# A two-block decoder in one kernel: the first transfers and splits in smaller pieces, the first chunks serving both token tiles, small loads after chunk 9, the last token tile's left half first, two output queues

## The reference

```python
def _rmsnorm(t, g):
    t32 = t.astype(jnp.float32)
    t32 = t32 * lax.rsqrt(jnp.mean(t32 * t32, axis=-1, keepdims=True) + RMS_EPS)
    return t32.astype(t.dtype) * g

def _swiglu(t, w_gate, w_up, w_down):
    return (jax.nn.silu(t @ w_gate) * (t @ w_up)) @ w_down

# first steps of the first layer
f = _swiglu(_rmsnorm(h, ffn1_pre_g[l]), ffn1_w_gate[l], ffn1_w_up[l], ffn1_w_down[l])
h = h + 0.5 * _rmsnorm(f, ffn1_post_g[l])
...
# last steps of the last layer
h = h + conv_ffn(rms_norm(h, ffn_norm[layer]), ffn_w_up[layer], ffn_conv[layer], ffn_w_down[layer])
...
return rms_norm(h, final_norm)
```

## Time and profile before

| | |
|---|---|
| timed runs | 1845.45 us median (1845.1 to 1845.69) |
| the profiled execution: span, first to last instruction | 1842.3 us (its time beyond the span is not listed) |
| TensorE busy | 1829.0 us, 99% |
| VectorE, ScalarE, GpSimd busy | 1287.1, 1090.7, 205.1 us |
| the chain that ended last | TensorE 96%, VectorE 2%, ScalarE 1% |
| DMA | 333.94 MB, mean 181 GB/s |

### The profile page before, as it was taken

One profiled execution on the slowest core, in us unless ns is written; L12 is line 12 of the kernel. 1 busy time (PEld: TensorE's weight loads), 2 busy tenths in 40 slices (PEclk: granted clock), 3 DMA queues, 4 the chain that ended last, 5 costly groups with the idle time before them and its releaser, 6 DMA issues.

```text
span 1842.3 us, 28823 instructions
## 1 busy us (share of the span) xinstructions
PE 1829.0 (99%) x10951; PEld 1633.5 (89%) x10951; DVE 1287.1 (70%) x2041; ACT 1090.7 (59%) x1885; POOL 205.1 (11%) x158
## 2 busy tenths in 40 slices
PE   8999999999999999999999999999999999999998
PEld 7888999998888888888999888888889998989997
DVE  6775747787777568755777788755768765768763
ACT  7665545555666466645555657655557654757653
POOL 0220001110022002200011102210002210001210
PEclk9999999999999999999999999999999999999999
DMA  9755565455576558664654548654747654537663
GB/s 268 216 186 183 172 194 171 140 158 176 173 225 192 189 148 233 186 193 139 196 176 143 186 146 230 193 190 144 226 139 215 187 195 155 173 115 205 198 192 103
DMA packets 435721, 333.94 MB, mean 181 GB/s; under 512 B 25338, under 2 KB 381312, under 8 KB 435584
## 3 DMA queue, kind: packets, MB, share of 16 engines
q1 hardware_dynamic: 435008, 331.57, 59.7%
q10 hardware_dynamic: 576, 0.53, 0.1%
HBM read 330.97 MB, written 1.05 MB: 180 GB/s over the span
## 4 chain that ended last, share of the span: by engine, by line
PE 96%; DVE 2%; ACT 1%; issue 0%; DMA 0%; ACTq 0%
PE bank L1759 16%; PE bank L1736 15%; PE bank L1738 15%; PE bank L1737 15%; PE bank L1747 7%; PE bank L1761 7%; PE bank L1748 7%; PE bank L1749 7%; PE bank L1765 2%; PE bank L1758 1%; DVE wlo L1106 1%; PE bank L2017 0%; DVE U L1159 0%; PE bank L2083 0%; PE bank L2088 0%; PE bank L2054 0%
## 5 line engine op out<-in xcount | busy, mean ns | idle before, releaser
L1106 DVE TENSOR_TENSOR wlo<-raw,whi 128x1024 fp32r<-128x1024 f32 (+3 forms) x637 | 760.9, 1202 | 286.3 <-ACT whi L578 276.8
L578 ACT ACTIVATE whi<-raw 128x1024 fp32r<-128x1024 f32 (+3 forms) x637 | 645.6, 1023 | 324.6 <-PE bank L1738 247.9
L1759 PE MATMUL bank<-U,whi 128*128 128x512 f32 x1280 | 439.2, 395 | 0.2 <-DVE wlo L1106 0.2
L1761 PE MATMUL bank<-U,wlo 128*128 128x256 f32 x1120 | 314.6, 281 | 0.0
L1747 PE MATMUL bank<-U,whi 128*128 128x256 f32 x1024 | 289.2, 282 | 0.0
L1748 PE MATMUL bank<-U,whi 128*128 128x256 f32 x1024 | 286.1, 279 | 0.0
L1749 PE MATMUL bank<-U,wlo 128*128 128x256 f32 x1024 | 286.0, 279 | 0.0
L1759 PEld LDWEIGHTS bank<-U,whi 128*128 128x128 f32 x1280 | 230.2, 188 | 42.9 <-DVE wlo L1106 0.7
L1736 PE MATMUL bank<-whi,U 128*128 128x384 f32 (+2 forms) x592 | 219.2, 370 | 2.7 <-DVE wlo L1464 2.1
L1736 PE MATMUL bank<-whi,hhi 128*128 128x512 f32 x560 | 219.3, 392 | 0.0
L1738 PE MATMUL bank<-wlo,hhi 128*128 128x512 f32 x560 | 218.1, 390 | 0.0
(11 more groups left out here) (309 smaller groups left out, 2367.4 us busy)
## 6 DMA issues: line engine op xcount, KB each, us to landing
raw<-in_ffn_w_up SPq DMA_DIRECT2D x351, 256.0 KB, 3.5
raw<-in_ffn_w_down SPq DMA_DIRECT2D x264, 256.0 KB, 2.9
raw<-in_ffn_w_gate SPq DMA_DIRECT2D x175, 256.0 KB, 3.4
raw<-in_w_gate SPq DMA_DIRECT2D x128, 192.0 KB, 2.9
raw<-in_w_in SPq DMA_DIRECT2D x80, 256.0 KB, 3.4
raw<-in_a_w_in SPq DMA_DIRECT2D x48, 256.0 KB, 3.2
raw<-in_w_mem_kv SPq DMA_DIRECT2D x32, 256.0 KB, 3.3
raw<-in_w_out SPq DMA_DIRECT2D x32, 256.0 KB, 3.1
```

What stands on the lines that cost most here:

```text
L578: act.activation(whi[n % SLOTS][:, 0:w], raw[n % RAW][:, 0:w], ACT.Copy).then_inc(hi_ready, 1)
L1106: dve.tensor_tensor(wlo[n % SLOTS][:, 0:w], raw[n % RAW][:, 0:w], whi[n % SLOTS][:, 0:w].bitcast(F32), ALU.subtract).then_inc(lo_ready, 1)
L1759: ins = pe.matmul(dst, wh, u2[:, k, :], start=(k == 0), stop=(k == KT - 1))
L1761: pe.matmul(dst[:, 0:TOK], wl, uhi[:, k, :], start=False, stop=False)
```

## The change

At the head:
- x comes in four pieces of 128 x 512. The order on SP is: identity, x tile 0 left, the second half of chunk 0, x tile 1 left, chunk 1, x tile 0 right, x tile 1 right, chunks 2 and 3. ScalarE loads the first half of chunk 0.
- The 16 small loads are issued after the DMAs of chunk 9. The ones are made by a memset of VectorE instead of a load.
- TensorE does the gains' transpose first, then 7 fillers, the transposes of x tile 0 left, 9 fillers, x tile 1 left; the right halves are transposed behind chunk 1.
- Chunks 0 to 3 are each used for both token tiles before the next one, and all four are split in halves of 512 columns. High and low parts of x are made two k at a time, and ScalarE reads a bank again (odd j) once VectorE is done with the two k before.
- Three load semaphores become one (`p_loaded`, 15 loads), and the counts of `lo_ready` and `hi_ready` follow the halves.

At the end, token tile 1 gets its left half from all four last chunks and then its right half; VectorE multiplies each half by the gain as soon as it is summed; after the reciprocal ScalarE scales columns 0 to 383 and stores them itself, VectorE columns 384 to 1023, which SP stores.

```diff
+        halves_done = lambda c: 2 * c + 2 if c < 4 else c + 5
+        LAST = 10
+        BY_ACT, BY_DVE = slice(0, 384), slice(384, DM)
...
                 if c >= RAW:
-                    sp.wait_ge(lo_ready, c - RAW + 2)
+                    sp.wait_ge(lo_ready, halves_done(c - RAW))
...
                     for s in range(2):
                         load(c + 2 * m + s, cols(w[s], KT, m * P, P))
+                    if m == 4 and after:
+                        after()
...
             sp.dma_start(ident, consts[:, C_ID:C_ID + P]).then_inc(cst_loaded, 16)
-            sp.dma_start(H[:, 0, :], A["x"][0, ts[0], :]).then_inc(x_loaded[0], 16)
+            load_x(0, 0)
             g0, u0 = A["ffn1_w_gate"][0], A["ffn1_w_up"][0]
+            chunk0 = raw[0][:, :].rearrange("p (k s n) -> p k s n", k=2, s=2)
+            for j, w in enumerate((g0, u0)):
+                sp.dma_start(chunk0[:, 1, j, :], w[P:2 * P, 0:256]).then_inc(w_loaded[0], 16)
+            load_x(1, 0)
             load(1, both(g0, u0, 2, 0))
+            load_x(0, 1)
+            load_x(1, 1)
             load(2, both(g0, u0, 4, 0))
-            sp.dma_start(H[:, 1, :], A["x"][0, ts[1], :]).then_inc(x_loaded[1], 16)
             load(3, both(g0, u0, 6, 0))
...
+            def small_inputs():
+                sp.dma_start(cst[:, C_GT:C_COS], consts[:, C_GT:C_COS]).then_inc(cst_loaded, 16)
+                sp.wait_ge(par_tp, 1)
...
+                if l == 0:
+                    ffn(0, 4, small_inputs)
...
@@ ScalarE
+            act.wait_ge(consts_ready, 2)
+            first_high(0, 0)
+            first_split(0)
+            first_high(1, 0)
+            first_high(0, 1)
+            first_high(1, 1)
+            first_split(1)
+            first_high(0, 2)
+            first_high(1, 2)
+            first_split(2)
+            first_high(0, 3)
+            first_high(1, 3)
+            first_split(3)
+            h_squares(0, 0)
+            split_to(4)
+            h_squares(0, 1)
             split_to(5)
...
+            act.activation(xn[:, 1, BY_ACT], xn[:, 1, BY_ACT], ACT.Copy, scale=stat(LAST, 1, RSTD)).then_inc(xn_done, 1)
+            act.wait_ge(xn_done, 4 * len(norm_at) + 1)
+            act.dma_start(out[0, ts[1], BY_ACT], xn[:, 1, BY_ACT]).then_inc(y_stored, 16)
...
@@ VectorE (the head in the same order as ScalarE, with first_low for first_high and h_bias for h_squares)
+            for nb in range(2):
+                wait_f(LAST, 1, nb)
+                dve.tensor_tensor(H[:, 1, half[nb]], bank[acc(LAST) + 2 + nb][:, :], H[:, 1, half[nb]], ALU.add).then_inc(h_ready, 1)
+                dve.wait_ge(h_ready, 4 * post(LAST) + 2 + nb + 1)
+                dve.tensor_tensor(xn[:, 1, half[nb]], H[:, 1, half[nb]], gpost[:, half[nb]], ALU.mult).then_inc(scaled, 1)
...
+            dve.tensor_scalar(xn[:, 1, BY_DVE], xn[:, 1, BY_DVE], stat(LAST, 1, RSTD), None, ALU.mult).then_inc(y_out, 1)
...
@@ TensorE
+                if b == 0:
+                    stream_turn(0, 1, 0)
                     for j in range(4):
+                        for t in range(TT):
+                            ins = token_block(c + j, j, t, 0, bank[t][:, :], 512, uh, ul, lambda k: first_operands(t, k))
...
+                            if j == 1:
+                                stream_turn(0, t, 1)
...
-            keep_busy(12)
             pe.wait_ge(pre_loaded, 16)
             pe.transpose(bank[0][:, 0:2 * KT], param_rows[0:2 * KT, 0, :], ident[0:2 * KT, 0:2 * KT]).then_inc(par_tp, 1)
-            keep_busy(4)
-            for nb in range(2):
-                stream_turn(0, 0, nb)
-            keep_busy(6)
-            pe.wait_ge(par_ready, 1)
+            keep_busy(7)
+            stream_turn(0, 0, 0)
+            keep_busy(9)
+            pe.wait_ge(consts_ready, 2)
```

More of the change, by code:

```diff
@@ L231, in program @@
         hi_ready, lo_ready, w_used = sem("hi_ready"), sem("lo_ready"), sem("w_used")
[L232 to L235, removed]
+        cst_loaded, pre_loaded, p_loaded = (sem(n) for n in ("cst_loaded", "pre_loaded", "p_loaded"))
+        x_loaded, x_rest, c0_loaded = [sem(f"x_loaded{t}") for t in range(TT)], sem("x_rest"), sem("c0_loaded")
+        gp_loaded, gb_loaded, rot_loaded = (sem(n) for n in ("gp_loaded", "gb_loaded", "rot_loaded"))
+        par_tp, consts_ready = sem("par_tp"), sem("consts_ready")
         f_full = sem("f_full")
@@ L401, in both, with ffn @@
                 return pieces
-            def ffn(f, skip=0):
+            def ffn(f, skip=0, after=None):
                 l, n = f // 2, f % 2 + 1
@@ L427, in _ @@
[L427 to L434, removed]
@@ L517, in _ @@
             conv_ffn(1)
-            for t in range(TT):
-                for nb in range(2):
[L520 to L526, removed]
+            for nb in range(2):
+                sp.wait_ge(y_out, nb + 1)
+                sp.dma_start(out[0, ts[0], half[nb]], xn[:, 0, half[nb]]).then_inc(y_stored, 16)
+            sp.wait_ge(y_out, 3)
+            sp.dma_start(out[0, ts[1], BY_DVE], xn[:, 1, BY_DVE]).then_inc(y_stored, 16)
             sp.wait_ge(y_stored, 64)
@@ L812, in mixer, with first_high, first_split @@
                 split_to(w0 + 3 + SLOTS)
[L815 to L827, removed]
+            def first_high(t, j):
+                if j % 2:
+                    act.wait_ge(u_done, 4 * (j - 1) + 2 * t + 2)
+                for k in (2 * j, 2 * j + 1):
+                    act.wait_ge(ut_full, (2 * (j // 2) + t) + 1)
+                    src = bank[acc(0) + 2 * t + j // 2][:, (k % 4) * P:(k % 4 + 1) * P]
+                    act.activation(uhi[:, k, ts[t]], src, ACT.Copy, scale=par[:, k:k + 1]).then_inc(uhi_done, 1)
+            def first_split(n):
+                for h, s in enumerate(half):
+                    if n == 0 and h == 0:
+                        act.wait_ge(c0_loaded, 32)
+                    else:
+                        act.wait_ge(w_loaded[n], 32)
+                    act.activation(whi[n][:, s], raw[n][:, s], ACT.Copy).then_inc(hi_ready, 1)
+                split[0] = n + 1
+            act.wait_ge(consts_ready, 2)
[14 more added lines that the diff above has]
+            h_squares(0, 1)
             split_to(5)
@@ L1456, in mixer, with first_low, first_split @@
                 split_to(w0 + 3 + SLOTS)
+            dve.memset(ones, 1.0).then_inc(consts_ready, 1)
             dve.wait_ge(par_tp, 1)
[L1460 to L1472, removed]
+            dve.tensor_copy(par[:, 0:2 * KT], bank[0][:, 0:2 * KT]).then_inc(consts_ready, 1)
+            def first_low(t, j):
+                dve.wait_ge(uhi_done, 4 * j + 2 * t + 2)
+                for k in (2 * j, 2 * j + 1):
+                    src = bank[acc(0) + 2 * t + j // 2][:, (k % 4) * P:(k % 4 + 1) * P]
+                    dve.scalar_tensor_tensor(ulo[:, k, ts[t]], src, par[:, k:k + 1], uhi[:, k, ts[t]].bitcast(F32),
+                                             ALU.mult, ALU.subtract).then_inc(u_done, 1)
+            def first_split(n):
+                for h, s in enumerate(half):
+                    dve.wait_ge(hi_ready, 2 * n + h + 1)
+                    dve.tensor_tensor(wlo[n][:, s], raw[n][:, s], whi[n][:, s].bitcast(F32), ALU.subtract).then_inc(lo_ready, 1)
+                split[0] = n + 1
+            first_low(0, 0)
+            first_split(0)
+            first_low(1, 0)
+            first_low(0, 1)
+            first_low(1, 1)
+            first_split(1)
+            first_low(0, 2)
+            first_low(1, 2)
+            first_split(2)
+            first_low(0, 3)
+            first_low(1, 3)
+            first_split(3)
+            h_bias(0, 0)
+            split_to(4)
+            h_bias(0, 1)
             split_to(5)
@@ L1712, in _ @@
             conv_ffn(1)
[L1714 to L1724, removed]
+            residual(LAST, 0, lambda nb: wait_f(LAST, 0, nb))
+            h_bias(LAST, 0)
+            h_rstd(LAST, 0)
+            dve.wait_ge(rstd_done, 2 * LAST + 1)
+            dve.wait_ge(gp_loaded, 16 * 7)
+            for nb in range(2):
+                dve.scalar_tensor_tensor(xn[:, 0, half[nb]], H[:, 0, half[nb]], stat(LAST, 0, RSTD), gpost[:, half[nb]],
+                                         ALU.mult, ALU.mult).then_inc(y_out, 1)
+            for nb in range(2):
+                wait_f(LAST, 1, nb)
+                dve.tensor_tensor(H[:, 1, half[nb]], bank[acc(LAST) + 2 + nb][:, :], H[:, 1, half[nb]], ALU.add).then_inc(h_ready, 1)
+                dve.wait_ge(h_ready, 4 * post(LAST) + 2 + nb + 1)
+                dve.tensor_tensor(xn[:, 1, half[nb]], H[:, 1, half[nb]], gpost[:, half[nb]], ALU.mult).then_inc(scaled, 1)
+                if nb == 0:
+                    h_bias(LAST, 1)
+            h_rstd(LAST, 1)
+            dve.wait_ge(rstd_done, 2 * LAST + 2)
+            dve.wait_ge(scaled, 4 * 6 + 2)
+            dve.tensor_scalar(xn[:, 1, BY_DVE], xn[:, 1, BY_DVE], stat(LAST, 1, RSTD), None, ALU.mult).then_inc(y_out, 1)
             assert split[0] == CHUNKS
```

(20 more changed lines are left out.)

91 lines of the change are left out of this document (52 added, 39 removed).

## The result

| | before | changed |
|---|---|---|
| timed runs, median | 1845.14 us (1844.59 to 1846.01, 9 runs) | 1850.1 us (1847.48 to 1851.95, 9 runs) |
| ratio to before | | 1.0027, 95% interval 1.0018 to 1.0036 |
| span of the profiled execution | 1842.3 us | 1848.3 us |
| mean granted clock | 0.999 | 0.998 |

The change made the kernel 5 us slower. The time lies above the predicted range, and "slower" had a chance of 0.05. The runs also spread over 4.5 us instead of 1.4.

A forecast was written before the change was run, and what follows sets the result against it. The prediction took TensorE as the bound, busy 1829.0 of 1842.3 us. It added +1.7 at chunk 9 and -0.25 in the tail, giving a span of 1843.75, plus 3.15 makes 1846.9 us; range 1843.6 to 1848.6.

The forecast's parts named there:

- chunk 10's delay: Weights for ScalarE: chunk 10 lands at 37.2 instead of 33.25 behind the small loads, 4.0 us later.
- the clock: Rival: TensorE's clock falls after the new idle times, one half-speed chunk costs 2.8 us, time 1849.7; chance 0.06.
- The chain: From SP's loads to TensorE: chunk 10's lateness makes chunk 9 start at 39.9, TensorE 1.7 us later than today.
- the bound of 5.6: Upper bound on chunk 10's delay: `mem` takes 6.2 us from issue to landing, chunk 10's 1.8 behind it.
- the 0.7 us of the output at the kernel's end: Time from first issue to bytes at the trace's end, used for `mem`, issued at 30.9.
- 35.2 + 1.8: Landing of chunk 10: `mem` ends at 35.2, chunk 10's bytes take 1.8, given as 37.2.
- The slack: Ahead of chunk 9: 2.3 us between VectorE's up sum at 35.9 and TensorE's start at 38.21.
- the step from chunk 10 to chunk 9: With chunk 10 4.0 us late against 2.3 us of slack, chunk 9 starts 1.7 us later.
- The head: Kernel start: first matmul at 7.7, 2.3 us earlier than 9.97, of which some 0.8 are left after the norm.
- the idle time ahead of chunk 2: TensorE idles 1.9 us ahead of chunk 2, waiting for its split behind ScalarE's wait for the last transposes.
- The tail: Kernel end: shorter last scaling and output on two queues give -0.25 us, bounds -0.9 to +0.2.
- The base: Timed median 1845.45 lies 3.15 us above the profiled span of 1842.3, taken as unchanged.

The follow-up runs named there:

- e2_before_late: The kernel before with only the 16 small loads moved behind chunk 9 and the ones made by a memset: 1849.99 us, ratio 1.0028.
- experiments 3 and 4: The two runs e3_mem_later and e4_bias_later, one load each moved behind chunk 23 in the changed kernel: 1845.3 us and 1846.94 us.
- e9_fill_both: The changed kernel with filler transposes in both new idle times, 16 ahead of chunk 2 and 32 ahead of chunk 9: 1847.97 us.
- e1_loads_early: The changed kernel with its 16 small loads back at their old place, between chunk 3 and chunk 4: 1845.16 us, ratio 1.0002.
- e3_mem_later: The changed kernel with the 1 MB load of `mem` alone moved on behind chunk 23: 1845.3 us, ratio 1.0004.
- e4_bias_later: The changed kernel with the 8 KB bias load alone moved on behind chunk 23: 1846.94 us, ratio 1.0017.
- e5_filler: The changed kernel with 32 filler transposes in the idle time ahead of chunk 9 only: 1848.8 us.
- a0_after: The changed kernel itself, unedited, measured again on the same chip as e9_fill_both: 1849.88 us.
- e7_spread: The changed kernel with small loads two at a time behind blocks 8 to 15, GpSimd's mask wait behind its first feed-forward: 1844.92 us, ratio 1.0001.

## Why the prediction was wrong

Two steps failed: the size of chunk 10's delay, and the clock, which the sum left at full speed.

- **Where the time would go was right.** The chain "16 loads on SP, chunk 10 late, ScalarE in order, VectorE's up sum, TensorE ahead of chunk 9" stands line by line in the trace, and e2_before_late shows that the loads' place is the whole loss.
- **Chunk 10's delay was mis-sized: "I take 4.0", measured 6.0** (39.27 for 33.25), even above the bound of 5.6. SP issued `mem` 0.8 later than I had it (31.71 for 30.9): it began later and the issues took longer. The larger part is, by an estimate from the rows of experiments 3 and 4, the time from that issue to the bytes. I took the 0.7 us of the output at the kernel's end; here DMA moved 53 and 199 GB/s at first, and over 300 only from 34.0 on, 2.3 us after the issue. The bias makes up some 0.8 of these 1.6 us; what the other 0.8 are stays open. The bytes of `mem` and chunk 10 then took about what I gave them (5.3 us to 39.27; I had 5.4). My sum also has a slip: 35.2 + 1.8 is 37.0 and not 37.2, so the terms gave a delay of 3.8.
- **The slack was misread.** I took the row at 38.21 for chunk 9's start and so 2.3 us of slack; it is 2.5 (35.90 to 38.45). With the measured 6.0 this gives 3.5 of later start, as the trace has it (41.97 for 38.45). So the step from chunk 10 to chunk 9 holds.
- **The clock failed as a term that the forecast put at nothing.** It was the rival that came true beside the forecast, not instead of it. Its price was 2.5 us in the profile and 1.9 in the medians with fillers. Without it the change costs 3.3 us (e9_fill_both), which on the 1845.14 of the result is 1848.4, at the upper end of the range (1848.6); with it, the change took 1850.1. I gave it 0.06 because 2.06 us of idle time today lowered nothing. One row of a profiled execution isn't a threshold: after 2.05 us the clock stayed up in the changed kernel's profile and fell in that of e1_loads_early. And with chunk 10 at 6.0 the idle time was 3.8 us, not 2.4. The Trainium skill ("TensorE: Matmul & The Clock Gate", section "HAM oscillation — how this bites in real kernels") says that long idle gaps put the array back to half speed; these traces agree, with 0.50 after 3.76 us, and show falls after 2.05 us too, shorter than the waits that the section describes; there the measurement decides. The price of one chunk at half speed (2.8) was about right (2.5).
- **The head.** First matmul predicted at 7.7, measured 8.22; the idle time ahead of chunk 2 predicted as 1.9, measured 2.05; the broadcast predicted to end at 25.5, measured 25.78. So 0.8 of gain was 0.4 (chunk 8 ends 0.39 earlier), and it was lost at chunk 9, as said.
- **The tail**: -0.25 predicted, -0.25 in the profile, -0.22 alone. The last bytes left in a stretch of 1.8 us at 291 GB/s, before and after. This is as the prediction's rule of the Trainium skill ("DMA: Bandwidth & Descriptors", section "Issuing engines are not separate DMA queues") has it: a second issuer saves issuing time only.
- **The base.** I added 3.15 us between span and time. In the runs that list both it is 1.8 (1850.1 and 1848.3): the profiled execution of before was a quick one, about 1 us under its median. Hence 6.0 in the span but 5.0 in the medians.

## What to carry to other kernels

A load that "isn't needed until later" still takes its place in an in-order queue: look at which load stands behind it, who stands in order behind that one, and how much slack the last of them has, and spread such loads over places with slack. Don't weigh a small load by its bytes alone: 8 KB cost 1.2 us here. Where TensorE gets a new idle time, sum it once with the clock up and once with it down: here a wait of 2 to 4 us grew by more than half. Runs that spread more than before can be a sign of it. And before a row of a timeline is taken for a start, look at how many instructions it merges.

## What the runs showed of the hardware

- The same idle time lowered the clock in some executions and not in others. Ahead of chunk 2 it was 2.05 us in seven profiles with the same code there, up to the loads' place in e1_loads_early. In those of e1_loads_early, e3_mem_later, e4_bias_later and e5_filler the clock fell to 1.2 GHz after it; in those of the changed kernel, a0_after and e7_spread it stayed at 2.4 GHz.
- These executions already differed at the start. The 9 fillers from about 6 us took 2.13 us in each of the four in which the clock fell later, and 1.33, 1.66 and 1.50 in the three others. The four are thus those that ran slow for longer at the start: 0.24 us a transpose, where the fillers ahead of chunk 9 in e9_fill_both took 0.11 each (3.65 for 32) at full clock. The clock column reads 1.00 in both places, so at the very start it doesn't tell. e9_fill_both started as slowly (2.13), had fillers in place of that idle time, and its clock stayed up. What sets the length of the slow start, and why the fall goes with it, no run here shows.
- The clock can fall after matmuls have begun again: in e1_loads_early they restarted at 17.96, the clock is 1.00 up to 19 us, and the lower level shows in the stretch from 19 on.
- Around the 8 KB broadcast in 64-byte pieces all DMA moved 53 GB/s for 1.5 us; without it, 139 in the matching stretch.
